# Twelve first weight sums per layer made in HBM by DMA instead of on VectorE, in a float32 trunk of two layers

## What is computed

```
x += rms(hybrid_mixer(rms(x)))          16 heads of three kinds, input and output projection
x += rms(memory_xattn(rms(x), rms(mem)))
u  = rms(x) @ w_up                      2048 x 8192
c  = causal depthwise conv of width 3 over u
x += rms((gelu(c_gate) * c_val) @ w_down)   w_down: 4096 x 2048
```

## Time and profile before

| | |
|---|---|
| median of 3 runs | 1966.92 us (1966.91 to 1967.28) |
| the profiled execution's own time | 1967.23 us |
| its span, first to last instruction | 1965.4 us |
| granted TensorE clock, mean | 0.999 |
| PE busy | 1952.6 us (99%) |
| DVE busy | 1506.6 us (77%) |
| ACT busy | 1138.2 us (58%) |
| POOL busy | 187.2 us (10%) |
| DMA | 393.94 MB, 200 GB/s over the span |

### The profile page before, as it was taken

One profiled execution on the slowest core, in us unless ns is written; L12 is line 12 of the kernel. 1 busy time (PEld: TensorE's weight loads), 2 busy tenths in 40 slices (PEclk: granted clock), 3 DMA queues, 4 the chain that ended last, 5 costly groups with the idle time before them and its releaser, 6 DMA issues.

```text
span 1965.4 us, 30737 instructions
## 1 busy us (share of the span) xinstructions
PE 1952.6 (99%) x10655; PEld 1680.0 (85%) x10655; DVE 1506.6 (77%) x2326; ACT 1138.2 (58%) x1770; POOL 187.2 (10%) x212
## 2 busy tenths in 40 slices
PE   9999999999999999999999999999999999999998
PEld 8888888888888888888888888888888888888886
DVE  7857777857777777788876577768587777778888
ACT  7655566657555555555566655556565555554654
POOL 0010000001222222200000000000012222222000
PEclk9999999999999999999999999999999999999999
DMA  8674558544656666576656444665446666565773
GB/s 319 200 204 155 170 211 241 198 152 169 202 192 207 198 206 200 203 274 240 220 150 229 153 155 160 213 218 196 155 153 205 203 201 209 188 205 210 267 251 135
DMA packets 111490, 393.94 MB, mean 200 GB/s; under 512 B 13140, under 2 KB 14560, under 8 KB 110048
## 3 DMA queue, kind: packets, MB, share of 16 engines
q1 hardware_dynamic: 105632, 368.36, 56.3%
q10 hardware_dynamic: 4448, 20.58, 2.7%
q0 software_dynamic: 1312, 3.70, 0.8%
HBM read 382.35 MB, written 10.24 MB: 200 GB/s over the span
## 4 chain that ended last, share of the span: by engine, by line
PE 98%; DVE 1%; issue 0%; ACT 0%; DMA 0%; DVEq 0%; SPq 0%; ACTq 0%
PE ps L971 24%; PE ps L974 12%; PE ps L881 12%; PE ps L883 11%; PE ps L882 11%; PE ps L893 11%; PE ps L896 5%; PE ps L1298 2%; PE ps L1297 2%; PE ps L1299 2%; PE ps L845 1%; PE ps L1248 1%; PE ps L1236 0%; PE ps L1234 0%; PE ps L1272 0%; PE ps L1260 0%
## 5 line engine op out<-in xcount | busy, mean ns | idle before, releaser
L1778 DVE TENSOR_TENSOR w_lo<-raw,w_hi 128x1024 fp32r<-128x1024 f32 (+2 forms) x660 | 778.6, 1187 | 323.0 <-ACT w_hi L1354 316.9
L1354 ACT ACTIVATE w_hi<-raw 128x1024 fp32r<-128x1024 f32 (+2 forms) x660 | 672.0, 1028 | 345.2 <-PE ps L974 219.7
L971 PE MATMUL ps<-h_t,w_hi 128*128 128x512 f32 x2032 | 639.0, 396 | 0.1
L974 PEld LDWEIGHTS ps<-h_t,w_lo 128*128 128x128 f32 x2032 | 382.1, 188 | 89.7
L974 PE MATMUL ps<-h_t,w_lo 128*128 128x256 f32 x2032 | 399.2, 278 | 0.0
L971 PEld LDWEIGHTS ps<-h_t,w_hi 128*128 128x128 f32 x2032 | 309.3, 189 | 0.3 <-DVE h_t L1796 0.3
L893 PE MATMUL ps<-h_t,w_hi 128*128 128x512 f32 x768 | 246.8, 403 | 0.0
L896 PEld LDWEIGHTS ps<-h_t,w_lo 128*128 128x128 f32 x768 | 144.3, 188 | 33.8
L2522 POOL TENSOR_SCALAR up_c<-up_u,cw 128x256 f32<-128x256 f32 x128 | 130.1, 1027 | 369.6 <-DVE up_u L2356 369.6
L896 PE MATMUL ps<-h_t,w_lo 128*128 128x256 f32 x768 | 151.2, 278 | 0.0
L883 PE MATMUL ps<-w_hi,act_t 128*128 128x512 f32 x320 | 124.5, 389 | 0.0
(11 more groups left out here) (372 smaller groups left out, 2838.4 us busy)
## 6 DMA issues: line engine op xcount, KB each, us to landing
raw<-stream SPq DMA_DIRECT2D x640, 512.0 KB, 4.3
comb<-comb_hbm SPq DMA_DIRECT2D x24, 512.0 KB, 4.8
comb_hbm<-comb_out ACTq DMA_DIRECT2D x14, 512.0 KB, 6.1
raw<-stream SPq DMA_DIRECT2D x24, 288.0 KB, 3.4
raw<-stream SPq DMA_DIRECT2D x16, 262.0 KB, 6.0
gain_a<-gains_in ACTq DMA_DIRECT2D x4, 1024.0 KB, 6.5
m_x<-mem_t_in ACTq DMA_DIRECT2D x2, 2048.0 KB, 11.6
x<-x_in SPq DMA_DIRECT2D x4, 512.0 KB, 13.4
```

What stands on the lines that cost most here:

```text
L971: pe.matmul(ps[:, 4 * half + nt, :], hi[:, cc, nt * P:(nt + 1) * P], h_t[:, c, :, :], start=(c == 0), stop=False, skip_group_check=True)
L974: mm = pe.matmul(ps[:, 4 * half + nt, SEQ:2 * SEQ], lo[:, cc, nt * P:(nt + 1) * P], h_t[:, c, 0, :], start=False, stop=(c == KC - 1), skip ...
L1354: act.activation(w_hi[:, slot, 0:width], raw[:, rslot, 0:width], ACT.Copy).then_inc(hi_ready, 1)
L1778: dve.tensor_tensor(w_lo[:, slot, 0:width], raw[:, rslot, 0:width], w_hi[:, slot, 0:width].bitcast(F32), ALU.subtract).then_inc(lo_ready, 1)
```

## The change

Sums 0 and 1 of each quad are no longer made by DVE. They are made in HBM, in a new tensor `b_hbm` with one block of 128 x 2 x 512 floats (512 KB) for each quad, by two DMAs that POOL issues: `sums_copy` copies the left halves of `ra` and `rb` from the stream, and `sums_add`, when the copy has landed, adds both halves of `rb` with an accumulating DMA. For eight quads this is done at points listed in `SUMS_EARLY`: when PE has used piece 48, 59, 70 and 81; then, after the factor row of the memory, piece 94, 105, 116 and 136. The last four are done inside the up-projection, the copy after an even group, the addition after the next odd one; for that POOL's loop is written out.

`psum_b` becomes two buffers that the quads take in turns, the second one in the upper half of `y_f`. ACT loads sums 0 and 1 of quad n into the buffer (`load_sums`, 512 KB): quad 0 ahead of split 4, quad 1 behind split 4, and quad n from 2 on behind ACT's part of split `SEVEN_AT[n - 2] + 5`. Quads 6, 8 and 10 go into buffer 0, which also holds the results of the first pass's merges, so their loads wait for both merges too and stand no earlier than behind split `down_end(1) + SPL + 1`, which is split 48. DVE keeps sums 2 and 3, at the same place in its program, and waits there for the load. SP no longer loads the left half of `rb` for eleven of the twelve quads of a layer.

```diff
@@ -83,6 +83,7 @@
 PASS_HEAD, PASS_TAIL = [1, 3], [[14, 15], [12, 14, 15]]
 PASS_MID = [[5, 0, 7, 2, 9, 4, 11, 6, 13, 8, 12, 10], [0, 5, 2, 7, 4, 9, 6, 11, 8, 13, 10]]
 COMBS = UPG // 2 - 1
+SUMS_EARLY = [(n, 48 + 11 * n) for n in range(4)] + [(4 + n, P_OUT + 6 + 11 * n) for n in range(3)] + [(7, P_MEMV)]
 
 DOWN_RAW, DOWN_SPLITS, DOWN_FREED = [], [], []
 for _q in range(2):
@@ -488,7 +489,7 @@
         gain_f = sb("gain_f", [P, D], 176 * K)
 
         comb = sb("comb", [P, 2, 4, 2, P], 80 * K, F32R)
-        psum_b = sb("psum_b", [P, 4, 512], 88 * K)
+        psum_b = [sb(f"psum_b{i}", [P, 4, 512], at) for i, at in enumerate((88 * K, 104 * K))]
         m1_s = sb("m1_s", [P, 512], 189 * K)
         y_f = sb("y_f", [P, 8, TB, 256], 96 * K)
         SCR = 176 * K
@@ -660,6 +661,9 @@
         comb_put = sem("comb_put")
         comb_got = [sem(f"comb_got{i}") for i in range(2)]
         b_sums = sem("b_sums")
+        b_put = sem("b_put")
+        b_made = sem("b_made")
+        b_got = [sem(f"b_got{i}") for i in range(2)]
         m1_copied = sem("m1_copied")
         odd_merged = sem("odd_merged")
         even_merged = sem("even_merged")
@@ -720,6 +724,11 @@
         def tail_at(s):
 
             return {P_DOWN + 4: 0, P_DOWN + 6: 2, P_DOWN + 10: 3, P_DOWN + 11: 4, P_DOWN + 12: 5, P_DOWN + 16: 6}.get(s, 1)
+
+        def first_sums(l, n):
+
+            m = l * len(SEVEN_AT) + n
+            return b_got[n % 2], 16 * (m // 2 + 1)
 
         def seven(s):
 
@@ -756,6 +765,7 @@
             return xo_t, [i], None
 
         bias_hbm0 = nc.dram_tensor("bias_hbm0", (4 * H_A, 4, 8 * P), F32, kind="Internal").ap()
+        b_hbm = nc.dram_tensor("b_hbm", (DEPTH * len(SEVEN_AT), P, 2, 512), F32, kind="Internal").ap()
         comb_hbm = nc.dram_tensor("comb_hbm", (DEPTH * COMBS, P, 4 * 2 * P), F32, kind="Internal").ap()
         f_hbm = nc.dram_tensor("f_hbm", (DEPTH, H_B, SEQ), F32, kind="Internal").ap()
         r_hbm = nc.dram_tensor("r_hbm", (DEPTH + 1, SEQ), F32, kind="Internal").ap()
@@ -812,7 +822,8 @@
 
                 for p in range(P_DOWN + RAW, NPIECES):
                     sp.wait_ge(lo_ready, raw_done(l, p - RAW))
-                    sp.dma_start(raw[:, p % RAW, :], stream[l * NPIECES + p]).then_inc(landed[p % RAW], 16)
+                    c = 512 if P_DOWN + DOWN_FREED[p - P_DOWN] - 1 in SEVEN_AT else 0
+                    sp.dma_start(raw[:, p % RAW, c:], stream[l * NPIECES + p][:, c:]).then_inc(landed[p % RAW], 16)
                     for n, s in enumerate(SEVEN_AT):
                         if p == max(P_DOWN + RAW, P_DOWN + DOWN_SPLITS[s - P_DOWN][4] + 2):
                             load_comb(n)
@@ -1415,10 +1426,13 @@
                         act.activation(w_hi[:, s % SPL, 0:512], raw[:, i % RAW, 512:1024], ACT.Copy).then_inc(hi_ready, 1)
                     else:
                         n = l * len(SEVEN_AT) + seven(s - 2 if kind == "B" else s - 3)
-                        act.wait_ge(b_sums, 3 * n + (1 if kind == "B" else 3))
+                        if kind == "B":
+                            act.wait_ge(*first_sums(l, n - l * len(SEVEN_AT)))
+                        else:
+                            act.wait_ge(b_sums, 2 * n + 2)
                         act.wait_ge(split_free, l * NSPLITS + s + 1)
                         c = 0 if kind == "B" else 2
-                        act.activation(w_hi[:, s % SPL, :], psum_b[:, c:c + 2, :].rearrange("p a n -> p (a n)"),
+                        act.activation(w_hi[:, s % SPL, :], psum_b[n % 2][:, c:c + 2, :].rearrange("p a n -> p (a n)"),
                                        ACT.Copy).then_inc(hi_ready, 1)
 
                 def split_dyn(p0, j, i, per):
@@ -1744,9 +1758,29 @@
                     up_split(UPG // 2 - 1, 1, j)
                     up_tail(UPG // 2 - 1, 0, j)
 
+                def load_sums(n):
+
+                    m = l * len(SEVEN_AT) + n
+                    if n < 2:
+                        act.wait_ge(*pieces_used(l, P_DOWN - 4 * (1 - n)))
+                        act.wait_ge(b_made, 16 * (l + 1) * len(SEVEN_AT))
+                    else:
+                        act.wait_ge(lo_ready, l * NSPLITS + SEVEN_AT[n - 2] + 4)
+                    if DOWN_SPLITS[SEVEN_AT[n] - P_DOWN][1] == 1 and n % 2 == 0:
+                        act.wait_ge(odd_merged, 2 * l + 1)
+                        act.wait_ge(even_merged, 2 * l + 1)
+                    act.dma_start(psum_b[n % 2][:, 0:2, :], b_hbm[m]).then_inc(b_got[n % 2], 16)
+
+                load_sums(0)
                 for s in range(P_DOWN + SPL, NSPLITS + (2 if l < DEPTH - 1 else 0)):
                     up_tail(UPG // 2 - 1, 1, tail_at(s))
                     split_down(s)
+                    if s == P_DOWN + SPL:
+                        load_sums(1)
+                    for n in range(2, len(SEVEN_AT)):
+                        merged = DOWN_SPLITS[SEVEN_AT[n] - P_DOWN][1] == 1 and n % 2 == 0
+                        if s == max(SEVEN_AT[n - 2] + 5, down_end(1) + SPL + 1 if merged else 0):
+                            load_sums(n)
                     if s == P_DOWN + 20:
                         act.wait_ge(act_ready, l * UPG + UPG)
                         act.wait_ge(comb_put, 16 * (l * COMBS + COMBS + 1))
@@ -1920,36 +1954,29 @@
                                           w_hi[:, s % SPL, 0:512].bitcast(F32), ALU.subtract).then_inc(lo_ready, 1)
                     else:
                         c = 0 if kind == "B" else 2
+                        n = seven(s - 2 if kind == "B" else s - 3)
                         dve.wait_ge(hi_ready, l * NSPLITS + s + 1)
-                        dve.tensor_tensor(w_lo[:, s % SPL, :], psum_b[:, c:c + 2, :].rearrange("p a n -> p (a n)"),
+                        dve.tensor_tensor(w_lo[:, s % SPL, :], psum_b[n % 2][:, c:c + 2, :].rearrange("p a n -> p (a n)"),
                                           w_hi[:, s % SPL, :].bitcast(F32), ALU.subtract).then_inc(lo_ready, 1)
 
-                def first_sums(s):
+                def other_sums(s):
 
                     ra, rb = [(P_DOWN + DOWN_SPLITS[s - P_DOWN + d][4]) for d in range(2)]
-                    assert ra % RAW + 1 == rb % RAW
                     n = seven(s)
-                    if n == 0:
-                        dve.wait_ge(*pieces_used(l, P_DOWN - 4))
-                    else:
-                        dve.wait_ge(lo_ready, l * NSPLITS + SEVEN_AT[n - 1] + 4)
+                    m = 2 * (l * len(SEVEN_AT) + n)
+                    sums = psum_b[n % 2]
+                    if n > 1:
+                        dve.wait_ge(lo_ready, l * NSPLITS + SEVEN_AT[n - 2] + 4)
+                    dve.wait_ge(*first_sums(l, n))
+                    dve.wait_ge(*raw_landed(l, rb))
+                    dve.tensor_tensor(sums[:, 2, :], sums[:, 0, :], raw[:, rb % RAW, 512:1024], ALU.add).then_inc(b_sums, 1)
+                    dve.wait_ge(b_sums, m + 1)
                     dve.wait_ge(*raw_landed(l, ra))
-                    dve.wait_ge(*raw_landed(l, rb))
-                    dve.tensor_tensor(psum_b[:, 0:2, :], raw[:, ra % RAW:rb % RAW + 1, 0:512],
-                                      raw[:, rb % RAW, :].rearrange("p (a n) -> p a n", n=512), ALU.add).then_inc(b_sums, 1)
-
-                def other_sums(s):
-
-                    ra, rb = [(P_DOWN + DOWN_SPLITS[s - P_DOWN + d][4]) % RAW for d in range(2)]
-                    n = 3 * (l * len(SEVEN_AT) + seven(s))
-                    dve.wait_ge(b_sums, n + 1)
-                    dve.tensor_tensor(psum_b[:, 2, :], psum_b[:, 0, :], raw[:, rb, 512:1024], ALU.add).then_inc(b_sums, 1)
-                    dve.wait_ge(b_sums, n + 2)
-                    dve.tensor_tensor(psum_b[:, 3, :], psum_b[:, 2, :], raw[:, ra, 512:1024], ALU.add).then_inc(b_sums, 1)
+                    dve.tensor_tensor(sums[:, 3, :], sums[:, 2, :], raw[:, ra % RAW, 512:1024], ALU.add).then_inc(b_sums, 1)
 
                 def merge_sums(q):
 
-                    w5, w7, x57 = [psum_b[:, c, :] for c in range(3)]
+                    w5, w7, x57 = [psum_b[0][:, c, :] for c in range(3)]
                     dve.wait_ge(*pieces_used(l, LAST_SEVEN[q] + 1))
                     dve.wait_ge(m1_copied, 2 * l + q + 1)
                     st.done(dve.tensor_tensor(w5, ps[:, 7, :], m1_s[:], ALU.subtract))
@@ -1962,8 +1989,8 @@
                     g = G_DOWN + 2 * q + 1
                     if q == 0:
                         dve.wait_ge(*pieces_used(l, GROUP_END[g]))
-                    dve.tensor_tensor(acc(l, g, 0), acc(l, g, 0), psum_b[:, 0, :], ALU.add)
-                    st.done(dve.tensor_tensor(acc(l, g, 1), acc(l, g, 1), psum_b[:, 2, :], ALU.add))
+                    dve.tensor_tensor(acc(l, g, 0), acc(l, g, 0), psum_b[0][:, 0, :], ALU.add)
+                    st.done(dve.tensor_tensor(acc(l, g, 1), acc(l, g, 1), psum_b[0][:, 2, :], ALU.add))
                     dve.sem_inc(odd_merged, 1)
 
                 def merge_even(q):
@@ -1971,7 +1998,7 @@
```

(39 more changed lines are left out.)

## The result

The changed kernel takes 1993.12 us (median of 4 runs, 1989.8 to 1996.5) against 1967.03 us before: 1.0133 times the time, with an interval of 1.0120 to 1.0145. That is 26 us slower, where I had forecast 5. It also spreads by 7 us from run to run, where the kernel before spreads by 0.4. The profiled execution is one of the shorter ones, 1990.07 us.

The account below looks back on a forecast made before the run. PE was taken as the bound. All terms cost 0 except quad 6's late load, 2.46 + 2.45 = 4.9 us, added to the 1966.9 us median: 1971.8 us, 0.25% slower, with the range given from 1967.5 to 1976.0 us.

Parts of the forecast that it names:

- What bounds the kernel: Whole execution: PE is the bound, in work for 1952.6 of 1965.4 us; everything else runs ahead of it.
- DVE's saving: Line 1938 goes, 24 instructions, some 29 us of DVE; PE waited for none, so cost 0.
- The early quads stand where POOL had nothing to do. Cost 0.: POOL's copies and additions in the up-projection and before: early quads fall in POOL's idle time, cost 0.
- the copy has 22 us to land: Up-projection: the addition waits for a copy issued one group earlier, leaving 22 us before POOL waits; cost 0.
- rival B: Up-projection: copies and additions hold up the stream; four quads a layer 1 us late give 1980 us; chance 0.07.
- the 19 us that I had worked out as their room: Up-projection stream: cost is 0 as long as a load lands within some 19 us.
- Quad 6: Down-projection: its load behind ACT's split 48 makes PE wait 2.46 us in layer 0, 2.45 in layer 1.
- The 3.2 us that I worked out: Quad 6's load: skill-based landing estimate, 2.0 us plus bytes at 436 GB/s; delay 0.9 us a layer.
- A: Rival: quad 6's load lands in 3.1 to 4.2 us; both layers cost 1.5 to 3.8 us; chance 0.34.
- C: Rival: nothing is late at quad 6, its loads landing in 2.3 us or issued earlier; 1966.9 us; chance 0.03.
- D: Rival: DVE's relief gains at the layer's turn, at most 1.5 us and other waits there; chance 0.04, including the unseen.
- a stall of 2.5 us is just short of this: Clock: PE stood still at least 2.8 us before it fell; a 3.8 us stall might lower it.

Follow-up runs that it names:

- The last experiment: Changed kernel with POOL's DMAs given partitions as slowest dimension and the first pass's merges put in the other buffer: 1966.92 us, 0.9999 times before.
- the experiment on shape: Changed kernel with only POOL's DMAs reshaped, copy with partitions slowest, addition as two DMAs of 128 rows: 1970.99 us, 1.0021 times before.

## Why the prediction was wrong

**What bounds the kernel, DVE's saving: right.** The last experiment takes 26 us of work off DVE and 0.2 us off the time, inside its interval.

**The step that failed: "The early quads stand where POOL had nothing to do. Cost 0."** POOL did have idle time there. But I gave the early quads no landing at all, and asked of it only in the up-projection, where "the copy has 22 us to land". Each addition waits for its copy and blocks POOL's program, and the chain of quads 4 to 7 has one end that is wanted: the blocks of x at 451 us. From 333 to 451 there are 118 us for four pairs, 29 us for each. For landings like those of the loads in the earlier trace rows, 3.0 to 12.6 us, that is plenty; the four took 25 to 42 us, and PE waited 16.3 us for x. I had said that no row shows such a DMA, and then bounded it only by what it might do to the stream (rival B). The same unknown had a second place to act: POOL's own queue. The first thing to do with an added wait is to list what stands behind it on its engine, and line 2560 stood there.

**The unknown landing.** I named the rule that speaks to it: the Trainium skill (page "DMA: Bandwidth & Descriptors", section on why a DMA increments its semaphore by 16) has the number of engines that a transfer uses divide its slowest dimension. The runs agree with it: an addition of 2 blocks lands in 38.0 us, one of 8 in 14.7, and one of 128 rows in 6.1 (each of two halves), and while PE stood still POOL's queue took 11.9% and 13.3% of the 16 engines' time, about two engines. I gave the rule a chance only as a way to starve the stream. The stream didn't starve: its loads went from 4.2 to 7.1 us in the median, 18.5 at worst, just short of the 19 us that I had worked out as their room, and PE has no wait on them in the changed kernel.

**Quad 6: the mechanism was right, its size was not.** Forecast 2.46 and 2.45 us, measured 0.6 and 1.9. The landing (4.3 and 5.6 us) was inside my bounds; the term that was mis-sized is the issue, by 1.4 us. From one pair of rows I took it that ACT issues a DMA right behind the start of the activation ahead of it. It issued 0.33 us before the activation ahead of that one had started. The 3.2 us that I worked out by the Trainium skill (page "DMA: Bandwidth & Descriptors", section on the anatomy of one DMA) come from a fit that the page gives for DMAs issued by GpSimd, and this load is ACT's. The changed kernel's 24 loads landed in 3.4 to 6.8 us, 3.6 in the median.

**Rivals and the clock.** A wanted landings of 3.1 to 4.2 us and C none that is late; both are refuted by the 4.3 and 5.6 us. That the two waits together, 2.5 us, lie inside A's 1.5 to 3.8 is luck, from the early issue. B had the right DMAs and the wrong victim. D is what the last experiment tests, and it finds nothing. On the clock I wrote that "a stall of 2.5 us is just short of this". That was wrong: a wait of 1.88 us at quad 6 was followed by some 3 us at 0.50, and so was one of 2.00 in the kernel with the load of quad 6 moved, while one of 2.38 us, with the copy alone in the new shape, was not. So the length of the wait alone doesn't settle it, and what does stays open. Half clock cost 2.6 us behind the stall of 16.3 us and 1.7 us behind quad 6.

**The time.** 1971.8 was forecast, 1993.1 measured. With POOL's chain cured (the experiment on shape) the change takes 1971.0 us, 3.9 us over the kernel before, of which 3.4 show as PE's two waits at quad 6. The forecast's own mechanism was sized at 4.9.

## What to carry to other kernels

When a change adds DMAs with a wait between them, follow the issuing engine's program to the next thing that another engine wants, and hold the whole chain of landings against it; idle time of that engine is not the measure. Give a DMA a long slowest dimension (here: partitions first, blocks second), and allow for a fast DMA behind a slow one on the same queue being as slow. And before anything, ask whether PE ever waits for the work that is taken away: here it waited 1.5 us for DVE at the turn of a layer and never for the sums, so little more than no change was to be had.

## What I had not expected of the hardware

- A 512 KB copy inside HBM in 2 blocks of 128 rows of 2 KB landed in 27.3 us in the median (17.3 to 43.2), the same bytes with the partitions first in 5.2 us. An accumulating addition: 38.0 us in 2 blocks, 14.7 us in 8 blocks of quarter rows, 6.1 us as two DMAs of 128 rows.
- A copy of the fast shape landed in 9.5 us with no addition ahead of it on POOL's queue, and the next one in 41.6 us behind a slow addition (one run).
- With DMAs of two blocks POOL's queue took only 11.9% and 13.3% of the 16 engines' time while nothing else ran: about two engines.
- The granted clock fell to 0.50 behind a wait of PE of only 1.88 us; behind a wait of 2.38 us in another kernel it stayed at 1.00.
- The load of quad 6 left ACT's queue 0.33 us before the start of the split ahead of its own (921.03 and 921.36), so two activations early; moving it in the program changed its issue only as far as the semaphores that it waits for allowed.
- The time of the changed kernel was uneven: 7 us between its runs, 2.5 us with the wide shapes, 0.5 us with the wide shapes and the merges moved.
